# One program block for a hybrid encoder kernel, with the attention's first scores placed in the last projection visit, and the state-space mixer's transfers cut into smaller pieces

## What is computed

```python
def mixer_layer(x, w, fox_attend, h0_re, h0_im, mem_k, mem_v):
    h = rms_norm(x, norm_g)
    fq, fk, fv, fg, ff, su, sg, mq, mg = split_columns(h @ w_in)
    fq, fk = rms_norm(fq, fox_q_norm), rms_norm(fk, fox_k_norm)          # 8 heads x 64
    logf = jax.nn.log_sigmoid(ff + b_forget)
    fox_out = fox_attend(fq, fk, fv, logf) * jax.nn.silu(fg)             # causal, decay from cumsum(logf)
    ssm_y, h_re, h_im = s5_mixer(su, h0_re, h0_im, ...)                  # diagonal complex state, gelu, GLU
    ssm_out = ssm_y * jax.nn.silu(sg)
    mem_out = memory_attention(rms_norm(mq, mem_q_norm), mem_k, mem_v) * jax.nn.silu(mg)
    mix = jnp.concatenate([fox_out, ssm_out, mem_out], axis=-1) @ w_out
    return x + mix, fk, fv, logf, h_re, h_im
```

## Time and profile before

| | us |
|---|---|
| median of 3 runs (1530.35 to 1531.13) | 1531.02 |
| the profiled execution | 1535.54 |
| its span in the profile | 1533.7 |
| PE busy (95% of the span) | 1452.1 |
| VectorE busy (56%) | 860.7 |
| ScalarE busy (47%) | 714.0 |
| GpSimd busy (14%) | 216.8 |
| block 1, to the last matmul of the projections | 814.3 |
| block 2, first score to last output product | 820.65 to 1528.35 |
| mean granted TensorE clock, share of 2.4 GHz | 0.988 |

### The profile page before, as it was taken

One profiled execution on the slowest core, in us unless ns is written; L12 is line 12 of the kernel. 1 busy time (PEld: TensorE's weight loads), 2 busy tenths in 40 slices (PEclk: granted clock), 3 DMA queues, 4 the chain that ended last, 5 costly groups with the idle time before them and its releaser, 6 DMA issues. The chain is left out here.

```text
span 1533.7 us, 28675 instructions
## 1 busy us (share of the span) xinstructions
PE 1452.1 (95%) x10318; PEld 1199.1 (78%) x10318; DVE 860.7 (56%) x1873; ACT 714.0 (47%) x1726; POOL 216.8 (14%) x294
## 2 busy tenths in 40 slices
PE   7999997999998989999997999999999999999998
PEld 7998766778777767777776878878778788788887
DVE  3689754682566776664334666667666666422221
ACT  5666422432433553344333666766667677400100
POOL 1110433100043342210001000000000003221110
PEclk9999998999999999999998999999999999999999
DMA  6785799696288587879976663261542602255543
GB/s 213 244 270 211 236 243 239 207 304 197 91 210 294 189 252 221 266 234 312 316 232 143 173 138 84 63 146 26 121 96 52 146 2 63 68 167 184 175 155 106
DMA packets 207676, 271.86 MB, mean 177 GB/s; under 512 B 73456, under 2 KB 147600, under 8 KB 203920
## 3 DMA queue, kind: packets, MB, share of 16 engines
q1 hardware_dynamic: 206496, 270.02, 60.8%
q10 hardware_dynamic: 1040, 0.00, 0.0%
HBM read 184.83 MB, written 83.90 MB: 175 GB/s over the span
## 5 line engine op out<-in xcount | busy, mean ns | idle before, releaser
L910 PE MATMUL in_g<-in_wh,in_xh 128*128 128x512 f32 (+2 forms) x904 | 334.1, 383 | 16.3 <-DVE in_wl L1478 5.8
L910 PE MATMUL in_g<-in_wl,in_xh 128*128 128x512 f32 (+2 forms) x904 | 323.5, 371 | 0.0
L2371 DVE TENSOR_REDUCE attn_tops<-attn_s 128x1 f32<-128x512 f32 (+3 forms) x288 | 173.4, 619 | 136.3 <-PE attn_s L2209 136.3
L2295 ACT ACTIVATE attn_probs<-attn_s,attn_negmax 128x512 f32<-128x512 f32 (+3 forms) x384 | 227.7, 605 | 38.5 <-DVE attn_negmax L2375 38.3
L910 PE MATMUL in_g<-in_wh,in_xl 128*128 128x512 f32 (+2 forms) x904 | 237.7, 382 | 1.4 <-DVE in_xl L1502 1.3
L910 PEld LDWEIGHTS in_g<-in_wh,in_xh 128*128 128x128 f32 x904 | 166.7, 190 | 53.9 <-issue 21.6
L2223 PE MATMUL attn_t<-all_ident,attn_probs 128*128 128x128 f32 x1216 | 190.7, 275 | 5.8 <-ACT attn_probs_turned L2305 4.3
L910 PEld LDWEIGHTS in_g<-in_wl,in_xh 128*128 128x128 f32 x904 | 166.8, 190 | 28.2
L910 PEld LDWEIGHTS in_g<-in_wh,in_xl 128*128 128x128 f32 x904 | 160.0, 191 | 35.6 <-issue 5.5
L2223 PEld LDWEIGHTS attn_t<-all_ident,attn_probs 128*128 128x128 f32 x1216 | 147.3, 141 | 40.2 <-issue 9.2
L2239 PE MATMUL attn_pv<-attn_probs_turned,attn_v 128*64 128x128 f32 x2176 | 134.6, 275 | 0.8 <-DVE attn_out L2406 0.7
(11 more groups left out here) (288 smaller groups left out, 2291.2 us busy)
## 6 DMA issues: line engine op xcount, KB each, us to landing
in_xu<-scratch_xt SPq DMA_DIRECT2D x87, 512.0 KB, 5.2
in_xl<-scratch_xt SPq DMA_DIRECT2D x34, 512.0 KB, 5.0
in_raw<-in_w_in SPq DMA_DIRECT2D x40, 256.0 KB, 5.6
scratch_xt<-in_xu SPq DMA_DIRECT2D x19, 512.0 KB, 5.3
scratch_xt<-in_xl SPq DMA_DIRECT2D x17, 512.0 KB, 6.2
scratch_k<-in_x_turned SPq DMA_DIRECT2D x17, 512.0 KB, 5.8
scratch_q<-in_x_turned SPq DMA_DIRECT2D x17, 512.0 KB, 5.2
in_x_turned<-in_x_prompt SPq DMA_DIRECT2D x16, 512.0 KB, 4.5
```

What stands on the lines that cost most here:

```text
L910: last = X.matmul(g_ps[b][:, 0:m], x, ws[:, c, w0:w0 + m], start=(c == 0 and h == 0 and ws is wh), stop=(c == KC - 1 and h == 1))
L2295: last = F(probs[:, s % 2, i, at:at + n, :], s_ps[g % RING][:, at:at + n, :], ACT.Exp, bias=negmax[:, s % 2, top:top + 1], accum_out=total)
L2371: V.tensor_reduce(tops[:, s % 2, i:i + 1], bank[:, 0:n, :].rearrange("p n k -> p (n k)"), AX.X, ALU.max).then_inc(s_top, 1)
```

## The change

1. **One block.** `before_attention` and `attention_and_output` no longer open blocks; they return one function for each engine, and `build` opens one block in which each engine runs the first and then the second. All semaphores belong to one `Place`, cleared once at the end. Most semaphores of the mixer and of the requests are cleared midway by GpSimd alone, once the requests' results are stored, and it then raises `s_cleared`.
2. **The first scores move.** The scores of attention round 0 (PE), their maxima (VectorE) stand behind part 0 of the last visit, the first two exponentials (ScalarE) behind its part 2. Buffers and PSUM banks are laid out so that they don't overlap with what the last visit still uses: the transposes' banks are those of `in_g`, so that the first `turn` waits for the last gate.
3. **Loads of head 0's values** wait for `s_cleared` and for the requests' stores, no longer for a meeting of all engines.
4. **The mixer's slots.** `s5_drive` and what follows starts 3 slots later; the scan's two halves share a slot from level 2 on, and 6 empty slots follow it, so that the later steps keep their slots. The eight `s5_y_out` stand in eight slots (before: two each in every second slot); `s5_y_in` is four transfers of half the size, and the gate's load four of a quarter (`s5_sg_in`), 3 slots apart. The GLU begins one slot later.
5. **`early_in`**: seven loads in seven consecutive visits of "gate", before in every second.

```diff
@@ state_steps
-    at += 6
+    at += 9
     for g in range(GROUPS // 2):
         main.put(at + g, "s5_drive", g)
...
             main.put(at, "s5_scan", up, k, half)
-            at += 1
+            at += half if k > 1 else 1
+    at += 6
...
+    for n in range(8):
+        main.put(at + n, "s5_y_out", n)
     for n in range(4):
-        main.put(at + 2 * n, "s5_y_out", n)
-    main.put(at + 12, "s5_y_in", 0)
-    main.put(at + 14, "s5_y_in", 1)
-    main.put(at + 8, "s5_y_out", 4)
-    at += 22
+        main.put(at + 10 + 2 * n, "s5_y_in", n // 2, n % 2)
+        main.put(at + 17 + 3 * n, "s5_sg_in", n // 2, n % 2)
+    at += 23
@@ before_attention
     for n in range(7):
-        beside[gate + 3 + 2 * n, 1] = [("early_in", n)]
+        beside[gate + 2 + n, 1] = [("early_in", n)]
+    beside[NV - 1, 0] = [("attention_scores",)]
+    beside[NV - 1, 2] = [("attention_exp",)]
...
+            pool.wait_ge(s_pv, 2 * DEC_BATCH)
+            pool.wait_ge(s_pread2, DEC_BATCH)
+            pool.wait_ge(s_mout, DEC_BATCH)
+            pool.wait_ge(s_wide, 32 * DEC_BATCH)
+            pool.wait_ge(K.s_early, 16 * 7)
+            nc.clear_and_free_semaphores(K.done.sems)
+            pool.sem_inc(K.s_cleared, 1)
@@ s5_gated on VectorE
-                        dve.wait_ge(s_yt, 16 * 3)
+                        dve.wait_ge(s_yt, 16 * 4)
+                    dve.wait_ge(s_sgin[m], 16 * 2)
@@ attention_and_output
+        def sync_program(sp):
+            sp.wait_ge(K.s_cleared, 1)
+            sp.sem_inc(K.s_entered, 1)
+            sp.wait_ge(*K.end_sample)
+            for end in K.end_turned:
+                sp.wait_ge(*end)
             load_values(sp, 0)
+            sp.wait_ge(*K.end_products)
             load_queries_keys(sp, 1)
             load_values(sp, 1)
+            sp.wait_ge(*K.end_gates)
+            for end in K.end_stores:
+                sp.wait_ge(*end)
...
+        def tensor_begin(pe):
+            pe.wait_ge(K.s_cleared, 1)
+            pe.sem_inc(K.s_entered, 1)
+            pe.wait_ge(*K.end_turns)
+            pe.wait_ge(*K.end_sample_read)
+            tensor_steps(pe, begin["scores"])
...
                 if what == "turn":
+                    if q == 0:
+                        pe.wait_ge(*K.end_gates)
@@ build
-        before_attention(nc, K, D, I, O)
-        with ExitStack() as behind:
-            b = Place(nc, behind, "wout")
+        sync_first, tensor_first, scalar_first, vector_first, gpsimd_first = before_attention(nc, K, D, I, O)
+        block = stack.enter_context(nc.Block())
...
+        @block.tensor
+        def _(pe):
+            tensor_first(pe)
+            K.rest[1](pe)
```

More of the change, by code:

```diff
@@ L1937, in attention_and_output @@
     order = attention_order(rounds)
+    begin = {"scores": [x for x in order if x[0:2] == ("scores", 0)], "exp": [x for x in order if x[0:2] == ("exp", 0)][0:2]}
+    order = [x for x in order if x not in begin["scores"] and x not in begin["exp"]]
     SLOTS = max(sum(len(r.blocks) for r in g) for g in groups)
@@ L2182, in _, with tensor_program, tensor_steps @@
                 sp.wait_ge(s_yst[u], 16 * ((TILES + 1 - u) // 2))
[L2184 to L2185 removed]
+        def tensor_begin(pe):
[4 more added lines that the diff above has]
+            tensor_steps(pe, begin["scores"])
+        def tensor_program(pe):
+            tensor_steps(pe, order)
+        def tensor_steps(pe, steps):
             X = nc.tensor
[L2187 removed]
+            for what, s, *rest in steps:
                 if what == "scores":
@@ L2274, in _, with scalar_begin, scalar_program, scalar_steps @@
                     last.then_inc(s_g[h], 1)
-        @block.scalar
-        def _(act):
+        def scalar_begin(act):
+            act.wait_ge(K.s_cleared, 1)
+            act.sem_inc(K.s_entered, 1)
+            act.wait_ge(*K.end_sample)
+            act.wait_ge(*K.end_split)
+            scalar_steps(act, begin["exp"])
+        def scalar_program(act):
+            scalar_steps(act, order)
+        def scalar_steps(act, steps):
             F = nc.scalar.activation
-            for what, s, *rest in order:
+            for what, s, *rest in steps:
                 if what == "exp":
@@ L2347, in _, with vector_begin, vector_program, vector_steps @@
                     G.tensor_tensor(at[:, 0, :], at[:, 0, :], at[:, 1, :], ALU.mult).then_inc(s_mix, 1)
-        @block.vector
-        def _(dve):
+        def vector_begin(dve):
+            dve.wait_ge(K.s_cleared, 1)
+            dve.sem_inc(K.s_entered, 1)
+            dve.wait_ge(*K.end_sample)
+            vector_steps(dve, begin["scores"])
+        def vector_program(dve):
+            vector_steps(dve, order)
+        def vector_steps(dve, steps):
             V = nc.vector
-            for what, s, *rest in order:
+            for what, s, *rest in steps:
                 if what == "scores":
```

136 lines of the change are left out of this document (81 added, 55 removed).

## The result

| | before | changed |
|---|---|---|
| median of 4 runs, us | 1531.08 | 1519.01 |
| lowest to highest | 1530.35 to 1533.97 | 1517.45 to 1520.35 |
| the profiled execution (its span) | 1535.54 (1533.7) | 1520.35 (1518.6) |
| mean granted clock | 0.988 | 0.997 |

The ratio is 0.9915, with a 95% interval of 0.9903 to 0.9927: faster by 12.1 us, between the medians. The prediction said 22.8 us less and 1508.2 us; 1519.0 lies outside its range. The two profiled executions differ by 15.1 us in their spans: that of the kernel before lies 4.5 us above its median, that of the changed kernel 1.3 us.

The account below looks back on a forecast made before the run. TensorE, busy nearly all the time, was taken to bound the kernel; only its stops and slow-clock stretches could be won. Terms 9.7 + 6.9 + 5.7 + 0.5 = 22.8 us, off 1531.0, gave 1508.2 us; range 1501.5 to 1516.0.

Parts of the forecast that it names:

- The seam: Between projections and attention: removing TensorE's stop and the half clock behind it gains 9.7 us, between 7 and 12.
- (b): At the seam, the clock falls in two short stops behind the projections; seam gives 7, 1510.9 us; chance 0.10.
- (d): Late GpSimd clearing makes scores in the last visit hold up projections; seam's gain gone, 1517.9 us; chance 0.05.
- (c): Everything goes: on-chip transfers land before the fourth drive, both short seam stops vanish; 1501.7 us; chance 0.09.
- The drives: Mixer's drives in the "keys" pass, three slots later: TensorE's stop shrinks from 8.0 to 2.0 us; gain 6.9 us.
- the mixer's transfers: In the "queries" pass, smaller, spread transfers remove most of TensorE's stops and low clock; gain 5.7 us.
- (a): "Keys" pass: on-chip transfers come later as TensorE quickens, the stop stays 8 us; 1515.1 us; chance 0.12.
- (e): "Queries" pass: five more transfers each hold a visit's rows back 1 us; 1518.9 us; chance 0.04.
- The loads in every "gate" visit: "Gate" pass: head 0's extra loads are hidden by 9.6 us of cover and cost 0.
- (f): "Gate" pass: extra loads pile up, TensorE stops at 7 visits and runs at low clock; 1543 us; chance 0.03.
- The end: Behind the last issue: two clearings less gain 0.5 us, between 0 and 1.2.
- From the exponential of round 1 on: In attention, from 829.82 us on: the order stays as before; no gain or loss was counted there.

Follow-up runs that it names:

- e8: The kernel before with only the drives moved three slots later: 1527.26 us, ratio 0.9965.
- e2: The kernel before with the attention's on-chip buffers allocated in the changed kernel's order: 1535.20 us, ratio 1.0029.
- e12: The changed kernel with 192 bytes of padding ahead of the second head's queries: 1512.25 us, ratio 0.9880.
- e1: The kernel before with the score ring allocated last in PSUM, so the output product adds into other banks: 1532.24 us, ratio 1.0008.
- e4: The kernel before with only the change's hunks on the mixer and early_in; two blocks, barrier and attention as before: 1521.82 us, ratio 0.9938.
- e3: The changed kernel with w_out's low half back at its old address and the second head's loads behind the last gates: 1518.70 us, ratio 0.9919.
- e5: The changed kernel with the second head's queries and keys allocated first among the attention's buffers: 1518.42 us, ratio 0.9902.
- e10: The kernel of e5 with the samples' decay scan and stores two slots later, and 192 bytes of padding ahead of w_out's low half: 1506.40 us.
- e11: The changed kernel with later decay scan, output product's operands at old addresses, and the projections' stationary operands at the partition's foot: 1508.58 us, ratio 0.9867.
- e15: The kernel of e10 with rows of the projections' split weights 544 floats apart instead of 520: 1507.86 us, ratio 0.9843.
- e14: The changed kernel with 96 bytes of padding ahead of the second head's queries: 1515.96 us, ratio 0.9893.
- e7: The changed kernel without its early scores and exponentials, head 0's first scores coming behind the last visit: 1519.71 us, ratio 0.9920.

## Why the prediction was wrong

*The seam, 9.7: right.* 9.4 us from C to D, at full clock, with stops of 1.07 and 0.70 where 0.9 and 1.3 were forecast. Rivals (b) and (d) are out: the clock is 1.00 there, and the scores inside the last visit don't wait. So is (c): both short stops are there.

*The drives and the mixer's transfers, 6.9 and 5.7, together 12.6: the sum right against the same profile, the two terms not.* A to B fell by 12.5 us. A transpose that both kernels have lies between the two places, with 1156 matmuls of TensorE from A to it in either trace (first before, then changed):

```profile
428.69 0.66 PE L932 MATMUL in_tr<-all_ident,in_stage 128*128 128x128 f32 x4 [0.94 <-DVE in_stage L1552]
...
419.71 0.66 PE L943 MATMUL in_tr<-all_ident,in_stage 128*128 128x128 f32 x4 [0.95 <-DVE in_stage L1565]
```

From A to it 228.0 us became 218.8, behind it 132.5 became 129.1. So the drives gave 9.2 where 6.9 were forecast: stops of 1.67 and 1.51 came for the 2.0, but the low clock that the forecast left behind them (1.7) didn't come, and a stop of 0.6 at 291 went too. The transfers gave 3.4 where 5.7 were forecast: 0.6 were left for a late load, and the waits are 1.2 for rows and 1.9 in the GLU, which had none before. That the errors cancel is luck. Rival (a) is out: VectorE goes on at 262.00, before at 262.34. SP's slow issues (2.4 us for a load at 245 that takes 0.32 at 231) came at the same times in both kernels, so they don't hang on TensorE; that full rings cause them is a reading that no run tests. Further, e8 shows that from A to B the three slots alone bring nothing in its profile: I costed the scan's shared slots at nothing, and they are what keeps the gain.

Rival (e), the page's rule on small transfers (the Trainium skill, "DMA: Bandwidth & Descriptors", Rules for kernel authors), doesn't come in this kernel's time: five more transfers left waits of 1.2 and 1.9 us where there were 5.0. For a transfer alone the trace goes the page's way. The load of `D.sg` before and with the change, with size and median us from issue to landing:

```profile
s_room<-scratch_sg SPq DMA_DIRECT2D x1, 2176.0 KB, 12.1
...
s_room<-scratch_sg SPq DMA_DIRECT2D x4, 544.0 KB, 7.0
```

A quarter of the bytes takes over half the time. The order of SP's queue, shown with the change, says why it pays here: a visit's rows no longer stand behind the whole. That is read from the traces; no run cuts the transfers alone. The time that (e) gave, 1518.9 us, is next to the 1519.0 measured, and (d) gave 1517.9; neither came true, and the numbers agree by chance.

*The loads in every "gate" visit, 0: right*; there is no stop of PE in that pass in the changed kernel, and (f) is out. *The end, 0.5: wrong by 0.5.* From F to the end it takes 5.8 us in both: the clearings taken away bring nothing there.

*The step that failed* is "From the exponential of round 1 on (829.82) the order is as before", from which I costed attention and output at nothing. The order is as before, and attention is (490.4 and 490.2 us); the output product isn't, because the change also moved its operands on chip: **5.3 us**, half of the miss. The prediction has no term for the output product, and it gives no reason but the order for leaving it out. e2 shows it without the rest of the change, e12 takes it back with one line.

*The second error is in the base.* I took every term from an execution that lay 4.5 us above the median and then subtracted all of them from the median. Part of what it showed was its own: e1, the same work in the same order, ran from A to B in 358.6 us, 1.9 less, and to A in 0.8 less, and its profiled execution took 1532.71 us. The 1.9 fit the clock: after the stop at 224 the window 226 to 228 is at 0.50 before and in the changed kernel, and at 1.00 in e1. With e2, which has the same order there and took 357.2 us, the gain from A to B is 9.3, 10.6 or 12.5 us by the execution compared with, and e4, which has this part alone, gained 9.6 us at the medians (interval 6.4 to 12.6) where 12.6 were forecast. Against e1's span of 1531.0 the changed kernel's 1518.6 is 12.4 us less, as the medians say. The 10.4 us between 22.8 and 12.4 then lie so: 5.3 in the output product, 1.9 from A to B, 1.0 up to A (where the changed kernel's 200.9 is among the longest of 199.3 to 202.3), 1.4 in the wait at L1096, 0.5 in the tail, and 0.3 in the rest. Only the first of these is tied to its cause by experiments; the others compare single executions, and what part of them is chance stays open.

The range reached to 1516.0 for rivals that spoke of waits, transfers and the clock. None spoke of instructions that become slower where they stand.

## What to carry to other kernels

When a change reorders allocations, compare the mean and the start-to-start distance of the commonest instructions before and after, also in stages that the change doesn't touch; a line of padding tells whether the addresses do it. A step that waits for many small transfers is cheapest to mend by moving it later in its engine's order, but only if what comes behind it in the chain has slack to take the delay, or gets it back as the scan did. Subtract terms from the execution that they were read in, and look at a second profile of the same work before calling the difference to the median an offset. A sum can come out right from terms that are each wrong: check the terms.

## What the runs showed of the hardware

The pace of a 128x512 matmul in fp32r depended on where its operands lay within a partition: 0.2273 us from start to start against 0.2340, with nothing but 192 bytes of padding changed (e12), and with values between (0.2292, 0.2322) for other paddings. Both the moving and the stationary operand count (e3, e5, e10). The score ring's banks don't (e1). I found no rule that fits all, and the projections' matmuls stayed at 0.2315 to 0.2323 us in all kernels (e11 and e15 moved their operands).

The granted clock doesn't follow from the length of one stop. Around and behind the stop at L1096 two windows of 4 us have a mean of 0.70 and 0.50 after 3.83 us in the changed kernel, and of 0.85 and 0.72 after 2.04 us in e14, but it stayed at 1.00 after 3.28 us in e12 and 2.55 us in e7. Nor does it at the stop at 224: it fell after 2.08 us in the kernel before and 1.93 in the changed one, and stayed at 1.00 after 2.00 in e4. For e12 the two windows at the stop at L1096 are

```profile
567.00:571.00 4.00, 2.54 (x14) 2.17 (x15) 3.25 (x8) 1.38 (x3) 1.97 (x3) 1.00 1.01 356
571.00:575.00 4.00, 4.00 (x24) 3.35 (x23) 2.91 (x8) 2.37 (x6) 0.23 (x2) 1.00 1.04 318
```

From B to C the changed kernel took 131.8 us, e14 128.8 and e12 128.4, with the same order there: the length of this stop and the clock behind it are part of why that stretch varied.
